# Third attention layer: unscaled probabilities, the output of the value product scaled by rows of inverses that pass through memory

## The reference, cut to what matters

```python
def chunk_band_attention(q, k, v, n_prev, bias, sinks):   # third layer: n_prev=8, 16 heads, sinks=None
    ...
        s = jnp.einsum('bqhgd,bjhd->bhgqj', q_c, k_c).astype(F32) * scale
        s = s + bias.reshape(Hkv, G, CHUNK, band).astype(F32)
        valid = key_idx >= pad - start
        s = jnp.where(valid, s, -jnp.inf)
        p = jax.nn.softmax(s, axis=-1)
        o = jnp.einsum('bhgqj,bjhd->bqhgd', p.astype(v.dtype), v_c)
    ...
def odd_mixer(y, w_in, w_out, rel_table):
    ...
    o = chunk_band_attention(q, k, v, C_PREV_CHUNKS, bias, None)
    return o.reshape(B, S, C_DIM) @ w_out
```

## Time and profile before

| | us |
|---|---|
| median of the runs | 2072.51 (2071.71 to 2074.53, 3 runs) |
| the profiled execution's own time | 2075.14 |
| its span, first to last instruction | 2073.3 |
| PE busy (x10366) | 2055.2 |
| DVE busy (x1927) | 1180.8 |
| ACT busy (x1163) | 759.5 |
| POOL busy (x138) | 123.8 |

### The profile page before, as it was taken

The page is one execution under the profiler, slowest core; times in us unless marked ns, Lnnn a source line. Parts: engine busy times, 40 slices in busy tenths (PEclk is TensorE's granted clock), DMA queues, the critical chain, the costliest instruction groups (busy, mean ns, idle before and its releaser), DMA issues.

```text
span 2073.3 us, 27109 instructions
## 1 busy us (share of the span) xinstructions
PE 2055.2 (99%) x10366; PEld 1689.7 (81%) x10366; DVE 1180.8 (57%) x1927; ACT 759.5 (37%) x1163; POOL 123.8 (6%) x138
## 2 busy tenths in 40 slices
PE   9999999999999999999999999999999999999999
PEld 7888888778888888988788888888876688888887
DVE  5444433786444433487778666633668877666433
ACT  5222222354322222463454322222557753222222
POOL 0000000400000000000002000000413120000001
PEclk9999999999999999999999999999999999999999
DMA  8322233312222222331221322233347622232222
GB/s 255 121 98 101 76 99 108 130 47 96 86 101 101 96 69 98 116 102 62 92 82 62 101 101 101 76 99 109 103 128 166 158 78 102 101 101 95 72 96 82
DMA packets 78300, 210.90 MB, mean 102 GB/s; under 512 B 46192, under 2 KB 49568, under 8 KB 61840
## 3 DMA queue, kind: packets, MB, share of 16 engines
q1 hardware_dynamic: 72896, 184.04, 28.0%
q0 software_dynamic: 2992, 12.31, 2.1%
q10 hardware_dynamic: 2336, 13.52, 1.8%
HBM read 195.08 MB, written 7.38 MB: 98 GB/s over the span
## 4 chain that ended last, share of the span: by engine, by line
PE 88%; DVE 6%; ACT 3%; issue 1%; DMA 1%; POOL 0%; SPq 0%; ACTq 0%; DVEq 0%
PE ps L1184 28%; PE ps L1185 28%; PE ps L1186 28%; ACT weigh L561 2%; DVE w_lo L1629 1%; PE ps L684 1%; DVE weigh L576 1%; DVE halves L583 1%; PE ps L666 1%; ACT w_hi L1621 1%; PE ps L651 1%; DVE weigh L593 1%; DMA h<-in_x_t 0%; ACT x_split L1707 0%; PE ps L1171 0%
## 5 line engine op out<-in xcount | busy, mean ns | idle before, releaser
L1184 PE MATMUL ps<-x_split,w_hi 128*128 128x512 f32 (+1 forms) x1774 | 697.6, 393 | 1.2 <-DVE x_split L1667 1.2
L1186 PE MATMUL ps<-x_split,w_lo 128*128 128x512 f32 (+1 forms) x1774 | 688.3, 388 | 0.0
L1185 PE MATMUL ps<-x_split,w_hi 128*128 128x512 f32 (+1 forms) x1774 | 688.1, 388 | 0.0
L1611 ACT ACTIVATE w_hi<-raw 128x2048 fp32r<-128x2048 f32 (+3 forms) x144 | 242.2, 1682 | 495.2 <-PE ps L1186 492.3
L1184 PEld LDWEIGHTS ps<-x_split,w_hi 128*128 128x128 f32 x1774 | 333.3, 188 | 79.2 <-issue 12.5
L1639 DVE TENSOR_TENSOR w_lo<-raw,w_hi 128x2048 fp32r<-128x2048 f32 (+3 forms) x144 | 287.9, 1999 | 179.7 <-ACT w_hi L1611 179.2
L1186 PEld LDWEIGHTS ps<-x_split,w_lo 128*128 128x128 f32 x1774 | 333.2, 188 | 68.5
L1185 PEld LDWEIGHTS ps<-x_split,w_hi 128*128 128x128 f32 x1774 | 333.5, 188 | 66.5 <-issue 1.0
L1184 PE MATMUL ps<-act,w_hi 128*128 128x512 f32 (+1 forms) x1026 | 376.9, 367 | 3.4 <-DVE w_lo L1629 3.1
L1185 PE MATMUL ps<-act,w_hi 128*128 128x512 f32 (+1 forms) x1026 | 372.9, 363 | 0.0
L1186 PE MATMUL ps<-act,w_lo 128*128 128x512 f32 (+1 forms) x1026 | 372.7, 363 | 0.0
(11 more groups left out here) (248 smaller groups left out, 1760.3 us busy)
## 6 DMA issues: line engine op xcount, KB each, us to landing
raw<-in_w_up SPq DMA_DIRECT2D x87, 1024.0 KB, 4.9
raw<-in_w_down SPq DMA_DIRECT2D x29, 768.0 KB, 4.2
raw<-in_w_in SPq DMA_DIRECT2D x20, 1024.0 KB, 4.9
raw<-in_w_down SPq DMA_DIRECT2D x29, 640.0 KB, 3.8
raw<-in_w_out SPq DMA_DIRECT2D x8, 1024.0 KB, 4.9
raw<-in_w_in ACTq DMA_DIRECT2D x8, 1024.0 KB, 5.5
skew<-scratch POOLq DMA_DIRECT2D x1, 5120.0 KB, 32.4
biases<-skew POOLq DMA_DIRECT2D x16, 256.0 KB, 4.3
```

Of the source, the lines that this page charges most:

```text
L1184: pe.matmul(own, hi, rhs_hi, start=start, stop=False)
L1185: pe.matmul(own, hi, rhs_lo, start=False, stop=False)
L1186: return pe.matmul(own, lo, rhs_hi, start=False, stop=stop)
L1611: eng.activation(w_hi[:, w], raw[:, w], ACT.Copy).then_inc(hi_rounded, 1)
```

## The change

In the third layer the probabilities are no longer multiplied by the inverses. The halves are copied as soon as the exponentials are there. The reciprocals come after that copy and go into a small table `OUT_INV`, for two pairs of heads. After the last step of a pair, SP writes the table to memory (128 partitions by 8 numbers, each of 4 bytes, into a tensor `factors`); one transpose later it reads the two rows of 512 inverses back, each copied to 64 partitions, into `shifted` or `ssum`. DVE then multiplies the output in PSUM by that tile into `mix_raw`, which lies where `mix_lo` lies; ACT makes `mix_hi` from `mix_raw`, after its exponentials instead of before them; DVE makes `mix_lo` a slot later (for the last pair, in the same slot). PE may write a PSUM bank again as soon as `mix_raw` is made. The clearing of `ssum` moves from the start of out3 to the end of its woven part. In the first two layers the four transposes of the values, with ACT's copy, come two products later.

```diff
+        mix_raw = at("mix_raw", [P, KD * T], F32, act_at + 36 * ROOM)
...
+        OUT_INV = tiny[:, 48:64]
+        factor_rows = (shifted[:, 2:2 + T], ssum[:, :])
...
                 if s == 0 and c >= 2:
-                    pe.wait_ge(w_mix, c - 1)
+                    pe.wait_ge(w_mixed, c - 1)
...
+        def inverses_of(c):
+            return OUT_INV[:, c % 2 * 2 * NB:(c % 2 + 1) * 2 * NB].rearrange("p (h n) -> p h n", n=NB)
+
+        def factors_out_sp(sp, c):
+
+            sp.wait_ge(w_inverted, NPARTS * (c + 1))
+            if c >= 2:
+                sp.wait_ge(w_mixed, c - 1)
+            rows = factors[c % 2 * 2:c % 2 * 2 + 2, :].rearrange("h (n q) -> q h n", q=P)
+            sp.dma_start(rows, inverses_of(c), allow_slow_non_contiguous=True).then_inc(f_written, 16)
+
+        def factors_in_sp(sp, c):
+
+            sp.wait_ge(f_written, 16 * (c + 1))
+            for hh in range(2):
+                row = factors[c % 2 * 2 + hh:c % 2 * 2 + hh + 1, :]
+                sp.dma_start(factor_rows[c % 2][64 * hh:64 * hh + 64, :], row.to_broadcast([64, T])).then_inc(f_landed[c % 2], 16)
...
-            c, s = divmod(i - 7, NPARTS)
-            if s == 0 and 0 <= c < KD:
-                eng.wait_ge(w_weighed, NPARTS * (c + 1))
-                eng.activation(chunk(mix_hi, c), pair_bank(c), ACT.Copy).then_inc(w_mix_hi, 1)
             if 0 <= i < STEPS:
...
+            c, s = divmod(i - 7, NPARTS)
+            if s == 0 and 0 <= c < KD:
+                eng.wait_ge(w_mixed, c + 1)
+                eng.activation(chunk(mix_hi, c), chunk(mix_raw, c), ACT.Copy).then_inc(w_mix_hi, 1)
...
-                link(eng.reciprocal(INV[:, part_col(u, n=rows)], ROW[:, part_col(u, n=rows)]))
-                for part, (n, at_, n_keys) in enumerate(own):
-                    for hh in range(2):
-                        p = weigh_at(u, hh)[:, at_:at_ + n_keys]
-                        ins = eng.tensor_scalar(p, p, INV[:, part_col(u, part, hh)], None, ALU.mult)
-                ins.then_inc(w_normed, 1)
-                eng.wait_ge(w_normed, u + 1)
...
                 eng.tensor_copy(to, words).then_inc(w_halved, 1)
+                if s == 0 and c >= 2:
+                    eng.wait_ge(f_written, 16 * (c - 1))
+                sums = ROW[:, part_col(u, n=rows)].rearrange("p (n h) -> p h n", h=2)
+                eng.reciprocal(inverses_of(c)[:, :, own[0][0]:own[0][0] + len(own)], sums).then_inc(w_inverted, 1)
...
             if s == 0 and 0 <= c < KD:
+                eng.wait_ge(w_weighed, NPARTS * (c + 1))
+                eng.wait_ge(f_landed[c % 2], 32 * (c // 2 + 1))
+                eng.tensor_tensor(chunk(mix_raw, c), pair_bank(c), factor_rows[c % 2], ALU.mult).then_inc(w_mixed, 1)
+            if s == 1 and 0 <= c < KD or s == 0 and c == KD - 1:
                 eng.wait_ge(w_mix_hi, c + 1)
-                eng.tensor_tensor(chunk(mix_lo, c), pair_bank(c), chunk(mix_hi, c).bitcast(F32), ALU.subtract).then_inc(w_mix, 1)
+                eng.tensor_tensor(chunk(mix_lo, c), chunk(mix_raw, c), chunk(mix_hi, c).bitcast(F32), ALU.subtract).then_inc(w_mix, 1)
...
                     for u in range(STEPS):
                         slot_sp(sp, u)
+                        c, s = divmod(u, NPARTS)
+                        if s == 0 and c:
+                            factors_in_sp(sp, c - 1)
+                        if s == NPARTS - 1:
+                            factors_out_sp(sp, c)
+                    factors_in_sp(sp, KD - 1)
...
-                    if g == end - 14:
+                    if g == end - 12:
...
-                    link(eng.memset(ssum[:, :], 0.0))
                     for g in range(1, KD * KD // 2 + 1):
...
+                    link(eng.memset(ssum[:, :], 0.0))
                     break_out_dve(st, BARRIERS[st.name])
```

More of the change, by code:

```diff
@@ L166, in repeat, with build @@
         body(i)
-def build(nc, x_t, vecs, weights, mixer_consts, pool_tab, small_consts, pool_w, sinks, rel_bias, out_t, scratch, skew, stop=None):
+def build(nc, x_t, vecs, weights, mixer_consts, pool_tab, small_consts, pool_w, sinks, rel_bias, out_t, scratch, skew, factors, stop=None):
     names = [s.name for s in STAGES]
@@ L330, in build @@
         w_probs = sem("w_probs")
-        w_normed = sem("w_normed")
+        w_inverted = sem("w_inverted")
+        f_written = sem("f_written")
+        f_landed = [sem(f"f_landed{k}") for k in range(2)]
+        w_mixed = sem("w_mixed")
         w_halved = sem("w_halved")
@@ L2615 @@
     skew = nc.dram_tensor("skew", (16, P * (5 * P + 1)), F32).ap()
+    factors = nc.dram_tensor("factors", (4, T), F32).ap()
     build(nc, ap["x_t"], ap["vecs"], {s.name: ap[f"w_{s.name}"] for s in STAGES}, ap["mixer_consts"], ap["pool_tab"],
-          ap["small_consts"], ap["pool_w"], ap["sinks"], ap["rel_bias"], out_t, scratch, skew, stop=STOP)
+          ap["small_consts"], ap["pool_w"], ap["sinks"], ap["rel_bias"], out_t, scratch, skew, factors, stop=STOP)
     r = run(nc, [{f"in_{n}": v for n, v in arrays.items()}], core_ids=[0])
```

## The result

The changed kernel takes 2104.45 us (median of 6 runs, 2098.05 to 2113.76) against 2073.41 us (6 runs) of the kernel before, measured beside it: a ratio of 1.0155, with a 95% interval of 1.0128 to 1.0181. The forecast was 2065.1 us, with a range from 2062.8 to 2070.8. The execution that was profiled is the fastest of the six, 2098.05 us with a span of 2096.3 us, so it shows 23 us of loss over the 2073.3 us of before, and the median some 6 more.

A forecast was written before the change was run, and what follows sets the result against it. PE was taken as the bound, busy 99% of the span, made to wait by a DVE and ACT loop. Savings of 1.85 + 2.11 + 1.7 + 1.7 = 7.4 us turned 2072.51 into 2065.1 us, range 2062.8 to 2070.8.

The forecast's parts named there:

- What the loop holds: Third layer's attention steps on DVE and ACT: a cycle shrinks from 17.58 to 14.6 us, below PE's 16.96.
- gains 1 to 4: The four savings in PE's waits and clock, 7.4 us in sum.
- gains 2 and 3: End of the third layer's attention: PE's 2.11 us wait for weights goes, and 1.7 us of half clock behind it.
- gain 1: Third layer's attention cycles: PE's first wait for `ring` goes and slow cycles fall to 16.96 us, 1.85 us saved.
- gain 4: Values' transposes: two products later, PE no longer waits there, 1.7 us saved.
- B: Third layer's attention: `mix_hi` behind the exponentials delays late weights; only gain 1 and gain 4 come, 2068.9 us, chance 0.13.
- E: Attention loop: shorter, but PE still waits for something unseen; time within 1 us of 2072.5, chance 0.05.
- The write, 3.9 us, hidden: Inverses' write on SP's queue: taken as a median transpose, 3.9 us between 1.8 and 6.1, and hidden in a steady cycle.
- Rival D: SP's queue: SP waits for a slow write with transposes behind; 2083.9 us at 18.8, outweighing gains from about 14.5, chance 0.08.
- Rival C: Attention's end: last pair's inverses could be 1.3 us late, stopping PE, perhaps 1.7 more by clock; 2068.1 us, chance 0.16.
- cover of 8.7 us: Last pair: the write may take 8.7 us if it runs beside the last transpose.
- The estimate of 74 us: Inverses' write: nineteen times the median transpose, some 74 us, a loss far over 100 us; set aside for its 4 KB.

The follow-up runs named there:

- e2: The changed kernel without the write and reads of the inverses, so the attention isn't normalised; 2067.25 us, ratio 0.9970.
- e3: The changed kernel with the same 4 KB written as 128 pieces of 32 bytes, inverses in the wrong order; 2067.11 us, ratio 0.9969.
- e5: The changed kernel with the inverses written as 256 pieces of 16 bytes and read with a stride by DVE, everything computed; 2066.86 us, ratio 0.9967.
- e1: The kernel before with only the values' transposes two products later; 2072.02 us against 2074.05, ratio 0.9993.
- e4: The changed kernel with the two reads of the inverses one transpose later in SP's queue; 2115.49 us, ratio 1.0206.
- e7: The changed kernel with the 4-byte write in place but never read back, so SP never waits for it; 2100.05 us, ratio 1.0133.

## Why the prediction was wrong, point by point

**What the loop holds, and gains 1 to 4.** Right. `e2`, `e3` and `e5` have all of the change's computation and are 6.8 to 7.0 us below before, where the sum said 7.4. In `e5` the cycles are 16.98 us from the start of the steady part (16.96 forecast), the 2.11 us wait for weights and the fall of the clock at the end are gone (gains 2 and 3), no wait for `ring` is left (gain 1), and `e1` gives the values' 1.5 to 2.0 us (gain 4). With that rivals B and E fall too. Applied to the median of 2072.51, the gain would have made 2065.6. The additional product, the copies beside it and the reads are hidden, as taken.

**The write, 3.9 us, hidden.** This is the step that failed, and in two ways. Its size: taken 3.9 us with bounds of 1.8 and 6.1, measured 11.9. The bounds came from rows that had only the queue, the byte count or the element size in common with the write; no row of before has a written piece of 4 bytes, and for such an operation the range should have stayed open upwards, into the chances. Worse is the second: the write was costed by its own landing alone. It was given cover (10 us until a transpose, 20 us until the inverses) as if nothing else would change. In fact it takes time from every transfer beside it, transposes, biases and weights, on every queue.

**Rival D.** Right in sign and wrong in mechanism. It had SP's wait for the write as the cause and 14.5 us as the point of decision; the write took 11.9, below that. By the rival's own sum this gives 2065.1 + 3.2 + 1.7 = 2070.0, and yet the loss was 31 us. `e4` (more transposes beside the write: worse) and `e7` (no wait: 4 us better) show that the wait is a small part at most. Two things of the kernel were also left out of it: DVE's `halves` of a step wait for the transpose of the step before the last (the 26.8 us above), so that a late transpose stops DVE as well as ACT; and the halved clock was priced at 1.7 us once, where it took 9.0. Its chance of 0.08 was the size of a mishap, though the largest unknown of the change lay there.

**Rival C.** Its sign did show: DVE stood 7.4 us for the inverses before the last `mix_raw`, and the last `mix_lo` kept PE 5.2 us. This is a quarter of the stops, and here the write's own landing counts. But in `e5` and `e3`, with a write of 2 us, it does not occur, and the forecast's cover of 8.7 us was enough.

**The Trainium skill's rule.** The prediction set aside the warning of the Trainium skill, "DMA: Bandwidth & Descriptors", section "Rules for kernel authors", because the write moves only 4 KB. The rule's direction agrees with the trace (11.9 us against 2.0 for the same bytes in pieces of 16). That such a transfer becomes one descriptor for each element agrees with the packets of the traces (87,899 in the changed kernel, 80,731 with 32-byte pieces, and 8 x (1024 - 128) = 7168 is the difference). But their number does not carry the case: 1024 pieces of 8 bytes, and 1024 of 4 bytes read, cost the kernel nothing, while 128 pieces written side by side cost all of it. The estimate of 74 us, worked out from the factor of the Trainium skill, was six times too much for the write, though "a loss" was the right sign.

## What to carry to other kernels

A small transfer must be judged by its pattern and by what it does to the transfers beside it, not by its bytes and its own landing. Where partitions write single 32-bit elements into a contiguous row in memory, arrange the row so that each partition writes 8 bytes or more, or lay the elements apart; here pieces of 16 bytes turned a loss of 31 us into a gain of 7 (elements apart were only written, not read back). And when an operation has no row in the trace, the sum needs a case in which it is the new bound, with a chance that fits how little is known.

## What the runs showed of the hardware

- Writes to memory of 4-byte pieces side by side, from 128 partitions: 128 of them (512 bytes) land in 9.5 us, 1024 in 11.2 to 11.9 (15.6 from ACT's queue). The same 128 pieces 512 bytes apart take 2.1 us, 16 side by side 2.0 us, 1024 pieces of 4 bytes in the reading direction 2.8 us. Of 8 bytes 512 take 4.6 us, of 16 bytes 256 take 2.0 us.
- One such write holds up all traffic of the core's DMA engines: little moves for some 11 us (32 GB/s from 1586 to 1597 in the run with one write), and transposes issued within 21 us of it take 14.0 to 27.2 us instead of 3.9. Its pieces have started within a microsecond. In the three us behind that the DMA share is 0.35 at 5 GB/s; from 1600 to 1620 it reads 1.20 at 85 GB/s, so there the engines count as busy while they move little. Moving the write to another queue does not help.
- The cause within the chip stays open. That pieces beside one another matter is shown; that several engines update the same few bytes of memory in turn would fit the pieces apart, but no trace shows which engine writes which piece, and 8-byte pieces side by side and 16 of 4 bytes cost nothing. Why a load asked for after the landing is still slow is open as well. How near pieces must lie, and whether it is the alignment of 4 bytes that counts, wasn't tried.
- Stops of PE can cost more than their length. In the changed kernel TensorE was granted 1.2 GHz for 20.5 us in four pieces behind stops, which made 20.8 us of stops 9.0 us dearer. In the run with one write the fall came inside the stop of 11.7 us, and only the 4 us that it outlasted the stop were paid for, with 2 us.
